# Normalisation hand-overs of a float32 transformer kernel: statistics per token, weight rooms of their own, residual additions on VectorE

## What is computed

```python
def rms_norm(x, gain, eps=1e-6):
    y = x * lax.rsqrt(jnp.mean(x * x, axis=-1, keepdims=True) + eps)
    return y * gain

# second block, layer l; attention is diff_attention in layer 0, forgetting_attention in layer 1
a = attention(rms_norm(h, norm_pre[l]))
h = h + rms_norm(a, norm_post[l])
f = conv_ffn(rms_norm(h, ffn_norm_pre[l]))
h = h + rms_norm(f, ffn_norm_post[l])
```

## Time and profile before

| | |
|---|---|
| median of 3 runs | 3218.62 us |
| the three runs | 3216.22, 3218.62, 3218.68 us |
| span of the profiled execution, first to last instruction | 3216.7 us |
| mean granted TensorE clock in it | 0.993 |
| TensorE matmul busy | 3158.3 us (98%) |
| VectorE, ScalarE, GpSimd busy | 1744.4, 1160.1, 534.5 us |

### The profile page before, as it was taken

How to read it: one execution, slowest core, us unless ns; L and a number is a source line. 1 busy time by engine, 2 the same in 40 slices (tenths; PEclk the granted TensorE clock), 3 DMA queues, 4 the chain that set the end, 5 groups by cost and what they waited for, 6 DMA issues and landing times.

```text
span 3216.7 us, 42242 instructions
## 1 busy us (share of the span) xinstructions
PE 3158.3 (98%) x14778; PEld 2537.6 (79%) x14778; DVE 1744.4 (54%) x2707; ACT 1160.1 (36%) x1880; POOL 534.5 (17%) x482
## 2 busy tenths in 40 slices
PE   8999999999999999999999999999999999999998
PEld 6888876788888888776888878668888886778887
DVE  4434477543445434585543453557656546586474
ACT  4323246322223222354322232644324335443242
POOL 0000336200020000265100030231000422310004
PEclk9999999999999999999999999999999999999999
DMA  4355331333333333321333323112333231223332
GB/s 122 97 143 148 95 108 36 89 97 93 98 98 93 104 91 106 80 60 47 94 104 90 108 76 118 47 55 77 107 88 102 66 103 40 60 72 104 92 96 81
DMA packets 528363, 288.01 MB, mean 90 GB/s; under 512 B 13603, under 2 KB 520198, under 8 KB 528256
## 3 DMA queue, kind: packets, MB, share of 16 engines
q1 hardware_dynamic: 523648, 273.32, 29.4%
q0 software_dynamic: 4608, 13.30, 1.4%
HBM read 284.30 MB, written 10.02 MB: 91 GB/s over the span
## 4 chain that ended last, share of the span: by engine, by line
PE 86%; DVE 7%; issue 3%; ACT 3%; POOL 1%; DMA 0%; DVEq 0%; ACTq 0%; POOLq 0%
PE bank L1905 66%; PE bank L1918 5%; PE bank L2075 3%; PE bank L2185 2%; PE bank L1935 2%; PE bank L2227 2%; PE bank L2250 1%; PE bank L2011 1%; PE bank L1964 1%; DVE w_lo L1293 1%; ACT w_hi L817 1%; PE bank L1983 1%; DVE scaled_g L1399 0%; DVE tap_g L1488 0%; DVE norm_t L1383 0%
## 5 line engine op out<-in xcount | busy, mean ns | idle before, releaser
L817 ACT ACTIVATE w_hi<-w_raw 128x1024 fp32r<-128x1024 f32 (+2 forms) x477 | 534.0, 1119 | 1419.3 <-PE bank L1905 718.8
L1905 PE MATMUL bank<-h_hi,w_hi 128*128 128x512 f32 x2420 | 949.2, 392 | 7.4 <-DVE h_lo L1323 3.7
L1905 PE MATMUL bank<-h_hi,w_lo 128*128 128x512 f32 x2420 | 942.4, 389 | 0.0
L1905 PE MATMUL bank<-h_lo,w_hi 128*128 128x512 f32 x2408 | 937.7, 389 | 0.0
L1293 DVE TENSOR_TENSOR w_lo<-w_raw,w_hi 128x1024 fp32r<-128x1024 f32 (+1 forms) x445 | 616.0, 1385 | 526.1 <-ACT w_hi L817 526.1
L1905 PEld LDWEIGHTS bank<-h_hi,w_hi 128*128 128x128 f32 x2420 | 453.7, 187 | 115.1 <-issue 14.7
L1905 PEld LDWEIGHTS bank<-h_hi,w_lo 128*128 128x128 f32 x2420 | 453.8, 188 | 95.9
L1905 PEld LDWEIGHTS bank<-h_lo,w_hi 128*128 128x128 f32 x2408 | 451.7, 188 | 95.5 <-issue 1.9
L1905 PE MATMUL bank<-act_hi,w_hi 128*128 128x512 f32 x924 | 360.3, 390 | 0.0
L1905 PE MATMUL bank<-act_lo,w_hi 128*128 128x512 f32 x924 | 360.0, 390 | 0.0
L1905 PE MATMUL bank<-act_hi,w_lo 128*128 128x512 f32 x924 | 359.9, 390 | 0.0
(11 more groups left out here) (333 smaller groups left out, 4160.8 us busy)
## 6 DMA issues: line engine op xcount, KB each, us to landing
w_raw<-in_ffn_w_gate_dram SPq DMA_DIRECT2D x88, 512.0 KB, 3.8
w_raw<-in_ffn_w_up_dram SPq DMA_DIRECT2D x88, 512.0 KB, 3.8
w_raw<-in_ffn_w_down_dram SPq DMA_DIRECT2D x64, 704.0 KB, 4.6
w_raw<-in_ffn_w_in_dram SPq DMA_DIRECT2D x88, 512.0 KB, 3.8
w_raw<-in_ffn_w_out_dram SPq DMA_DIRECT2D x32, 704.0 KB, 4.7
w_raw<-in_w_in_dram SPq DMA_DIRECT2D x34, 512.0 KB, 3.8
w_raw<-in_a_w_qkv_dram SPq DMA_DIRECT2D x24, 512.0 KB, 3.8
w_raw<-in_w_out_dram SPq DMA_DIRECT2D x16, 512.0 KB, 3.8
```

The source lines that it names most:

```text
L817: nc.scalar.activation(split_home(c)[0][:, 0:nk, 0:cols], raw[c % 2][:, 0:nk, 0:cols], ACT.Copy).then_inc(hi_ready, 1)
L1905: mm = nc.tensor.matmul(result(c)[0:cols, :], w[:, k, 0:cols], x[k], start=(k == 0 and n == 0), stop=(k == nk - 1 and n == 2))
```

## The change

1. Statistics per token. In `half_stat` the squares become the stationary operand and one column of `mean_p` (all 1/128) the moving one: two matmuls of one column for each block of 256 tokens in place of one with 256 columns. The result is 128 tokens on partitions by 2. Root and reciprocal are then taken of 128x2. VectorE puts the two columns on the diagonals of two 128x128 blocks (`half_diag`, two multiplications of `ident`), and TensorE spreads them over the partitions by a product of ones with 128x256 (`half_spread`, float32). The post factor is read by VectorE from PSUM, the next stage's is copied to `rstd` by ScalarE (`spread_copy`).
2. The spreads stand in TensorE's program: post first half at the ninth block of the last two units' second part, post second half ahead of block 6 of the next stage's first half, the next norm's first half behind its second half, its second half ahead of block 3 of unit c + 2. The post statistic of the second half moves from the end of `finish` to ahead of block 3 of the next stage's first half.
3. Units c and c + 1 of the three following stages get rooms of their own for the rounded weights and the rest (`home`), in the memory of the bias tables, so ScalarE's `hi` and VectorE's `lo` of them no longer wait for TensorE and are issued at the start of the hand-over. `hi(c + 2)` and `lo(c + 2)` are issued inside it. In `fox` GpSimd waits for two units before it writes that memory.
4. VectorE does the additions to `xres`, one iteration behind the scaling, in place of GpSimd.
5. The final transposes use banks 3, 4, 0, 1 in place of 3 to 6.

```diff
+        home = [[put(f"home_{part}{i}", [P, KT, P], bias_at + 4 * D * (2 * n + i), f32r) for i in range(2)]
+                for n, part in enumerate(("hi", "lo"))]
+        HOMES = {BASE[n] + i for n in HALVED for i in range(2)}
-        STAT_HALF = [STATB[:, HALF[0]], OUT[:, HALF[1]]]
+        STAT_TOK = [STATB[:, T // 2:T // 2 + 2], OUT[:, 0:2]]
+        SPREAD_POST = [bank[5][:, HALF[0]], bank[6][:, HALF[1]]]
+        SPREAD_NEXT = [STATB[:, HALF[0]], OUT[:, HALF[1]]]
...
-                    for half, tok in enumerate(HALF):
-                        for k in range(KT):
-                            if half == 0:
-                                pool.wait_ge(t_first, T_FIRST[name] + k + 1)
-                            else:
-                                pool.wait_ge(t_ready, T_FIRST[name] + k + 1)
-                            nc.gpsimd.tensor_tensor(xres[:, k, tok], xres[:, k, tok], norm_t[k % 4][:, tok],
-                                                    ALU.add).then_inc(x_done if half else x_first, 1)
...
-                nc.scalar.activation(rms[:, HALF[half]], STAT_HALF[half], ACT.Sqrt, bias=eps_c[:, 0:1],
-                                     scale=1.0 / n).then_inc(rms_ready if half else rms_first, 1)
+                nc.scalar.activation(norm_tok[:, int(event in BASE), 2 * half:2 * half + 2], STAT_TOK[half], ACT.Sqrt,
+                                     bias=eps_c[:, 0:1], scale=P / D).then_inc(rms_ready if half else rms_first, 1)
...
                 half_square(name, 0, 0)
+                hi(c)
+                hi(c + 1)
                 half_square(name, 0, 1)
-                half_root("post_" + name, D, 0)
-                hi(c)
+                half_root("post_" + name, 0)
                 half_square(name, 1, 0)
-                hi(c + 1)
-                half_square(name, 1, 1)
...
                         if half == 0 and k == 2:
-                            half_root("post_" + name, D, 1)
+                            half_square(name, 1, 1)
+                        if half == 0 and k == 4:
+                            half_root("post_" + name, 1)
+                        if half == 1 and k == 2:
+                            half_root(following, 0)
                         if half == 1 and k == 4:
-                            half_root(following, D, 0)
+                            hi(c + 2)
+                spread_copy(following, 0)
...
-                    nc.vector.reciprocal(dst, rms[:, HALF[0]]).then_inc(rstd_first, 1)
...
+                chain(nc.vector.reciprocal(tok[:, 2 * half:2 * half + 2], tok[:, 2 * half:2 * half + 2]))
+                for t in (2 * half, 2 * half + 1):
+                    ins = nc.vector.tensor_scalar(rms[:, P * t:P * (t + 1)], ident[:, :], tok[:, t:t + 1], None, ALU.mult)
+                ins.then_inc(diag_ready if half else diag_first, 1)
...
                 half_take(name, how, 0, 0)
+                lo(c)
                 half_take(name, how, 0, 1)
-                half_invert("post_" + name, 0)
-                half_take(name, how, 1, 0)
-                lo(c)
+                lo(c + 1)
+                half_diag("post_" + name, 0)
+                dve.wait_ge(rstd_first, HALF_ROOT["post_" + name] + 1)
...
+                        if 1 <= k <= KT:
+                            dve.wait_ge(t_ready if half else t_first, T_FIRST[name] + k)
+                            nc.vector.tensor_tensor(xres[:, k - 1, tok], xres[:, k - 1, tok], norm_t[(k - 1) % 4][:, tok],
+                                                    ALU.add).then_inc(x_done if half else x_first, 1)
+                        if half == 0 and k == 1:
+                            half_take(name, how, 1, 0)
+                        if half == 0 and k == 4:
                             half_take(name, how, 1, 1)
...
+                        if half == 0 and k == 8 and name in NEXT:
+                            half_diag("post_" + name, 1)
+                        if half == 1 and k == 7 and name in NEXT:
+                            half_diag(NEXT[name], 0)
...
+                        if half == 0 and k == 3:
+                            half_stat("post_" + before, 1, [b[:, HALF[1]] for b in sq_last])
+                        if half == 0 and k == 6:
+                            half_spread("post_" + before, 1)
+                        if half == 1 and k == KT:
+                            half_spread(name, 0)
...
-                    mm = nc.tensor.matmul(STAT_HALF[half], ones[:, :], b, start=(k == 0 and not summed),
-                                          stop=(k == (n or len(blocks)) - 1))
+                    for j in range(2):
+                        mm = nc.tensor.matmul(STAT_TOK[half][:, j:j + 1], b[:, P * j:P * (j + 1)], mean_p[:, 0:1],
+                                              start=(k == 0 and j == 0 and not summed),
+                                              stop=(j == 1 and k == (n or len(blocks)) - 1))
...
+            def half_spread(event, half):
+
+                pe.wait_ge(diag_ready if half else diag_first, (DIAG[event] if half else HALF_ROOT[event]) + 1)
+                mm = nc.tensor.matmul((SPREAD_NEXT if event in BASE else SPREAD_POST)[half], ones[:, :], rms[:, HALF[half]],
+                                      start=True, stop=True)
...
-                            if (half, s, k) == (1, 0, nk // 2):
+                            if (half, s, k) == (1, 0, 3):
                                 half_stat("post_" + name, 0, [b[:, HALF[0]] for b in sq_last])
+                            if half and s * nk + k == 8:
+                                half_spread("post_" + name, 0)
```

More of the change, by code:

```diff
@@ L167, in program @@
             HALF_ROOT["post_" + n], HALF_SQ["post_" + n] = len(HALF_ROOT), half_squares
+            DIAG["post_" + n] = HALF_ROOT["post_" + n]
             half_squares += 2
             X_FIRST[n] = KT * len(X_FIRST)
+    SPREAD_DONE = {(n, half): 2 * i + half + 1 for i, n in enumerate(HALVED) for half in range(2)}
     T_FIRST = {n: KT * i for i, n in enumerate(n for n in stages if n in CHAINED)}
@@ L763, in _ @@
                     pool.wait_ge(o_ready, OUTB["fox"])
+                    pool.wait_ge(mm_done, BASE["fox"] + 2)
                     chain(nc.gpsimd.memset(own_rows[:, :, :], 1.0))
@@ L1172, in _ @@
                     token_root()
-                hi(c + 2)
+                if name not in HALVED:
+                    hi(c + 2)
                 if name == stages[0]:
@@ L1377, in post @@
                     for k in range(KT + lag):
+                        if half and k == 0:
+                            if name not in NEXT:
+                                half_diag("post_" + name, 1)
+                            dve.wait_ge(rstd_ready, ROOT["post_" + name] + 1)
                         if k < KT:
@@ L1782, in _ @@
                     continue
-                lo(c + 2)
+                if name not in HALVED:
+                    lo(c + 2)
                 if name == stages[0]:
@@ L1893, in _, with gemm @@
         def _(pe):
-            def gemm(c, x_hi, x_lo, ready, count, j=0):
+            def gemm(c, x_hi, x_lo, ready, count, j=0, midway=None):
                 b = c % 2
@@ L1902, in gemm @@
                 for k in range(nk):
+                    if midway is not None and k == 3:
+                        half_spread(midway, 1)
                     pe.wait_ge(ready, count + k + 1)
@@ L1962, in half_block @@
                 cols = UNIT[c][1]
-                for n, (w, x) in enumerate(((w_hi, h_hi), (w_hi, h_lo), (w_lo, h_hi))):
-                    mm = nc.tensor.matmul(result(c)[0:cols, tok], w[c % 2][:, k, 0:cols], x[:, k, tok],
+                w_high, w_low = split_home(c)
+                for n, (w, x) in enumerate(((w_high, h_hi), (w_high, h_lo), (w_low, h_hi))):
+                    mm = nc.tensor.matmul(result(c)[0:cols, tok], w[:, k, 0:cols], x[:, k, tok],
                                           start=(k == 0 and n == 0), stop=(k == KT - 1 and n == 2))
@@ L1969, in half_stat @@
             def half_stat(event, half, blocks, at=0, n=None):
-                if half == 0 and at == 0:
+                summed = event in POOL_SUM
+                if half == 0 and summed:
                     stat_free(event)
-                summed = event in POOL_SUM
                 if summed:
@@ L1976, in half_stat @@
                         pe.wait_ge(ssq_ready, POOL_SUM[event] + 1)
-                    nc.tensor.matmul(STAT_HALF[half], ones[:, :], ssq[:, HALF[half]], start=True, stop=False)
+                    for j in range(2):
+                        nc.tensor.matmul(STAT_TOK[half][:, j:j + 1], ssq[:, P * (2 * half + j):P * (2 * half + j + 1)],
+                                         mean_p[:, 0:1], start=(j == 0), stop=False)
                 for k, b in enumerate(blocks, at):
@@ L2013, in finish @@
                         mm.then_inc(mm_done if half else half_done, 1)
```

(4 more changed lines are left out.)

56 lines of the change are left out of this document (34 added, 22 removed).

## The result

The changed kernel takes 3233.7 us (median of 13 runs, 3220.45 to 3243.6); the kernel before, beside it, 3217.19 us (13 runs, 3216.01 to 3218.68). The ratio is 1.0053, 95% interval 1.0043 to 1.0063: slower by some 16 us, outside the predicted range of 3207.5 to 3222.5 and close to the 3235 of the first rival. The scatter has grown from 2.7 to 23 us, and it goes with one number: the run of 3220.45 us has a mean granted clock of 0.993, that of 3233.7 has 0.988, that of 3243.6 has 0.984. The last is the profiled one (span 3241.8 us), so the trace shows the loss at its largest, and no trace of a middling run was kept.

A forecast was written before the change was run, and what follows sets the result against it. TensorE, busy 98% of the span, was taken as the bound. Hand-overs gain 5.8 us and the end 2.0, together 7.8, less 3.2 for the clock: 3218.6 - 4.6 = 3214.0 us, range 3207.5 to 3222.5.

The forecast's parts named there:

- the first rival: One-column statistics in the hand-overs keep TensorE's clock low: 16 us slower, 3235 us; chance 0.14.
- The clock: Low clock after TensorE's idle times in the new hand-overs: 1.6 us charged in two of three, 3.2 us.
- Thin matmuls keep the clock low: One-column products in the hand-overs hold the clock down until c + 2: 8 us a hand-over, 3235 us; chance 0.14.
- the part that it put under an "if": One-column records in the hand-overs also double in duration at low clock: 22 us more.
- the window 148.4 to 151.8: Earlier stretch of the kernel before: TensorE busy all 3.40 us at clock 0.99, then 0.5; cited as busy not enough.
- The rest of the sum: Gains at full clock: 5.8 us over three hand-overs and 2.0 us at the end, 7.8 us together.
- The faster rival: Clock stays high in the hand-overs: 3210.8 us, or 3207.8 us if weight loads hide too; chance 0.20.
- Additions on VectorE: VectorE's scaling, addition and `h_lo` in the hand-overs: 1.15 us an iteration instead of 1.28 us.
- Weight rooms: Moving `lo(c + 1)`, 1.75 us, out of the hand-over's pipeline, where it preceded TensorE's 1.85 us wait.
- The square's wait: TensorE waits 0.45 us for the second square in the last units of diff and fox, none in conv_0.
- the end itself: Last scalings and additions take eight iterations of 0.75 us; last addition at 3208.4 instead of 3210.43, 2.0 us gained.
- last addition 8 us before the end: Sign in the later profile that the forecast was right: the final residual addition ends 8 us before the span's end.

The follow-up runs named there:

- e1: Changed kernel with the statistic's moving operand 128 columns wide instead of one: 3208.89 us, ratio 0.9974 to the kernel before.
- e7: Changed kernel with 128-column statistics and the residual additions back on GpSimd: 3203.96 us, ratio 0.9961 to the kernel before.
- e10: e7 without the weight rooms, roundings and rests back where they stood before except `lo(c)`: 3221.12 us, ratio 1.0012 to the kernel before.

## Why the prediction was wrong

**The clock: the step that failed.** The text charged "1.6 us, six tenths of the 2.7 us that the clock cost this hand-over before, in two of the three: 3.2 us". That takes the low stretches to be set by idle time and scales them with it. The idle time came below the forecast (0.9, 1.05 and 0.75 us; 0.71, 0.78 and 0.50 came), but the length of a stretch was set by what ran behind: 37.5 and 41.0 us, and with the records widened (e1) none, behind the same three waits (0.70, 0.77 and 0.50 us). In place of 1.6 us the profiled execution lost 14.5 us in the first hand-over. The rival "Thin matmuls keep the clock low" described it and priced 3235 us against 3233.7. Its terms: 84 matmuls times 0.095 is 8.0 us and 0.9 for the spreads; the part that it put under an "if" and left out of the 3235, one-column records doubling, came true too, 0.36 to 0.71 us a block, 5.6 us for 16 blocks. The sum, 14.5 us, is the difference between the changed kernel's first hand-over and e1's, 39.21 less 24.71. That the median came near 3235 is luck: by its own words the doubling was worth 22 us more, and against that it happened in two hand-overs of three and, by the mean clocks of the runs, less in most of them than in the profiled one.

**Its chance.** It had 0.14. For it stood the window 148.4 to 151.8, all busy and followed by a low clock; against it were put arguments with no row behind them: that the new records load full weights, and that more than half of the hand-over is wide. e1 has the same loads, so they are no protection. But the window is a weaker witness than the text took it for. Its products, in the timeline of the kernel before, are narrow in rows and in weights (33 by 8), while the moving operand has 512 columns:

```profile
148.46 3.39 PE L2313 MATMUL bank<-onehot,table 33*8 33x512 f32 x12
```

It shows that a busy TensorE can lose the clock, not that a moving operand of one column does it. No row of before showed that.

**The rest of the sum, tested by e1.** With the clock up, c + 2 starts at 2188.52; 2188.5 was forecast, and the last units end 0.88 us later than before, for 0.89. From one stage to the next the gains are 1.5, 1.7, 2.2 and at the end 3.5 us, where 1.8, 2.2, 1.8 and 2.0 stood, the last without the low clock of the tail of before. Two errors inside cancel: a block of the statistic takes 0.36 us, not 0.44, and VectorE with 1.13 us an iteration is then the slower of the two, so TensorE waits instead. The faster rival's 3210.8 compares with 3208.9.

**Additions on VectorE.** "where it was 1.28 with the addition elsewhere" compared with the wrong kernel. The 1.28 came with the factor in SBUF; part 1 of the same change moved it to PSUM, and with that the iteration is 0.88 us with the addition elsewhere (e7). Part 4 was credited with 0.13 us an iteration and costs 0.25.

**Weight rooms.** Priced by the wait of 1.85 us, right in direction, far too low: e10 puts them at 17 us in the kernel with the short iterations. There 11.8 us of waits more cost 17 us, and low stretches come with them. What the rooms are worth in the kernel before was not run.

**Kept.** The square's wait (0.22 us in diff and 0.37 in fox for 0.45 forecast), root to diagonals without a gap, no wait on the diagonals in the hand-overs (the one of 2.0 us is at the end), the end itself (last scalings and additions of 0.73 us each pair, 0.75 forecast). The sign "last addition 8 us before the end" does not follow from the text's own sum: the last one ends 5.3 us before the end of the changed kernel, and 6.3 before.

## What to carry to other kernels

A reduction moved from a wide product to a one-column one saves little on TensorE here (0.36 for 0.43 us a block) and can cost the clock. In this kernel 128 columns of a constant matrix, with the first column read, cost no more and left the clock up. Read the granted clock by window, since the busy share is 98% in both kernels. Before pricing a move between engines, price it in the kernel with the other parts of the change in it; where a factor is read from, PSUM or SBUF, set the scaling's duration here, and the same move gained 3 us in one kernel and lost 5 in the other. The best version is e7, 3203.96 us: the change with 128 columns and with the additions left on GpSimd, 13 us under the kernel before and 30 under the changed one.

## What was not expected of the hardware

- TensorE busy without a gap for 35 us at 1.2 GHz (2168 to 2203 above). The Trainium skill, "TensorE: Matmul & The Clock Gate", section "Why this matters for your kernels", advises keeping TensorE busy without a break to get the full clock; these rows disagree, since busy with one-column records among wide products was not enough.
- At nearly equal idle time (5.1, 6.1 and 6.6 us of waits for `h_lo`, the most where the clock stayed up) and equal loads the clock's fate went by the width of the moving operand: low for 85, 27 and 0 us in the three hand-overs with 1, 32 and 128 columns (37.5 + 6.8 + 41.0; 10.2 + 6.8 + 10.2; none).
- Four records of a statistic take 0.36 us with one column and with 128 alike.
